# Attention units worked off in two halves, with value products between the turns, in a two-layer diffusion backbone kernel

## The reference, cut to what matters

```
o_b = softmax(q_b k_b^T) v_b            6 query heads on 2 key/value heads, 64 wide
o_c = rmsnorm((softmax(q_0 k_0^T) - lam * softmax(q_1 k_1^T)) v_c)    4 heads, 2 maps of 32
```

## Time and profile before

| What | us |
|---|---|
| median of 3 runs | 2925.51 (2918.04 to 2929.34) |
| the profiled execution, its own time | 2917.24 |
| its span, first to last instruction | 2915.6 |
| mean granted clock of TensorE in it | 0.903 of full speed |
| unit loop, layer 0 | 444.8 to 704.5 |
| unit loop, layer 1 | 1666.5 to 1929.9 |

### The profile page before, as it was taken

One profiled execution on the slowest core, in us unless ns is written; L12 is line 12 of the kernel. 1 busy time (PEld: TensorE's weight loads), 2 busy tenths in 40 slices (PEclk: granted clock), 3 DMA queues, 4 the chain that ended last, 5 costly groups with the idle time before them and its releaser, 6 DMA issues. The chain is left out here.

```text
span 2915.6 us, 46493 instructions
## 1 busy us (share of the span) xinstructions
PE 2488.3 (85%) x18972; PEld 2217.9 (76%) x18972; DVE 1454.1 (50%) x2077; ACT 1072.0 (37%) x1752; POOL 312.4 (11%) x334
## 2 busy tenths in 40 slices
PE   6995878776899999989949697777599999999993
PEld 4983655555899999989836565567499999999993
DVE  5675654555432223246656645543345555555556
ACT  4332244443322122143313535532235444444443
POOL 0064322000000000000643220000100000000002
PEclk8997986888999999999979868887699999999997
DMA  5324739101232222213146000010666765676664
GB/s 202 94 66 111 213 119 300 61 1 37 66 84 62 79 73 68 69 52 87 39 111 199 19 0 1 1 47 12 217 187 202 224 207 174 205 233 203 184 190 173
DMA packets 453114, 340.46 MB, mean 117 GB/s; under 512 B 90961, under 2 KB 421151, under 8 KB 451935
## 3 DMA queue, kind: packets, MB, share of 16 engines
q1 hardware_dynamic: 436383, 277.43, 32.9%
q10 hardware_dynamic: 11520, 41.95, 4.4%
q0 software_dynamic: 5056, 18.88, 1.7%
HBM read 287.68 MB, written 50.53 MB: 116 GB/s over the span
## 5 line engine op out<-in xcount | busy, mean ns | idle before, releaser
L2321 PE MATMUL ps<-h_hi,w_hi 128*128 128x256 f32 x1408 | 399.9, 284 | 5.6 <-DVE w_lo L2404 5.6
L2321 PE MATMUL ps<-h_lo,w_hi 128*128 128x256 f32 x1408 | 399.5, 284 | 0.0
L2321 PE MATMUL ps<-h_hi,w_lo 128*128 128x256 f32 x1408 | 399.4, 284 | 0.0
L2404 DVE TENSOR_TENSOR w_lo<-w_raw,w_hi 128x2048 fp32r<-128x2048 f32 (+1 forms) x180 | 309.2, 1756 | 120.6 <-ACT w_hi L2354 120.6
L2321 PEld LDWEIGHTS ps<-h_hi,w_hi 128*128 128x128 f32 x1408 | 271.0, 192 | 8.7 <-issue 6.0
L2321 PEld LDWEIGHTS ps<-h_lo,w_hi 128*128 128x128 f32 x1408 | 271.0, 192 | 2.8
L2321 PEld LDWEIGHTS ps<-h_hi,w_lo 128*128 128x128 f32 x1408 | 271.0, 192 | 0.0
L2354 ACT CAST w_hi<-w_raw 128x2048 fp32r<-128x2048 f32 (+1 forms) x180 | 256.6, 1474 | 2.6 <-DMA w_raw<-in_moe_w_down 2.6
L1829 DVE TENSOR_TENSOR p_lo<-ps,p_hi 128x512 fp32r<-128x512 f32 (+1 forms) x196 | 121.7, 632 | 136.5 <-ACT p_hi L1896 136.2
L1886 ACT ACTIVATE tm<-ps,tm 128x768 f32<-128x768 f32 (+1 forms) x140 | 111.3, 795 | 203.2 <-DVE tm L1824 203.1
L1824 DVE TENSOR_REDUCE tm<-ps 128x1 f32<-128x768 f32 (+1 forms) x140 | 113.1, 819 | 118.6 <-PE ps L1728 66.2
(11 more groups left out here) (427 smaller groups left out, 5624.6 us busy)
## 6 DMA issues: line engine op xcount, KB each, us to landing
w_raw<-in_moe_w_gu SPq DMA_DIRECT2D x182, 512.0 KB, 5.1
w_raw<-in_moe_w_down SPq DMA_DIRECT2D x91, 512.0 KB, 5.9
G_decay<-in_ada_w ACTq DMA_DIRECT2D x54, 512.0 KB, 4.7
w_ahead<-in_ffn_w_gu SPq DMA_DIRECT2D x44, 512.0 KB, 5.2
slots_h<-tm SPq DMA_DIRECT2D x13, 1024.0 KB, 11.1
slots_y<-tm SPq DMA_DIRECT2D x12, 1024.0 KB, 11.2
w_ahead<-in_ffn_w_down SPq DMA_DIRECT2D x16, 704.0 KB, 4.7
oA<-in_ada_w ACTq DMA_DIRECT2D x20, 512.0 KB, 5.0
```

Source lines behind the costliest of these rows:

```text
L2321: mm = pe.matmul(ps[:, j % 2, half * BLK:(half + 1) * BLK], gu(wt, j, half, k), x[:, k, :], start=(k == 0 and n == 0), stop=(k == KC - 1 a ...
L2404: dve.tensor_tensor(wlo[:, q, part], raw[:, q, part], whi[:, q, part].bitcast(F32), ALU.subtract).then_inc(s["lo_d" if down else "lo_u"], 1)
```

## The change

The unit's tiles get the order 1, 2, 3, 4, 0 (`order`). Tiles 1 and 2 are the first half, tiles 3 and 4 the second, each with its own half of `p_hi` and `p_lo` and its own half of the sums' bank; the context block has a place of its own behind both. The 12 products of 512 columns become 24 of 256 columns. In turn v, PE does the second half's products of unit v-1 and the first half's of unit v, two key blocks at a time, between turns and scores. `bring_out` waits for two halves. DVE and ACT orders follow; `probabilities` of a tile stands one tile later behind its scores. Beside that, `gdn` and `gdiff` are loaded in the preparing stage of attention into free columns of `mixed`, where `nlam` and `ro` now lie too, and `out_proj` copies `gdiff` into a buffer first.

```diff
-                    sp.dma_start(self.gdn[:], i["dn_norm"][l].partition_broadcast(P)).then_inc(s["par_in"], 16)
-                    sp.dma_start(self.gdiff[:], i["diff_norm"][l].partition_broadcast(P)).then_inc(s["par_in"], 16)
...
+                        sp.dma_start(gdn, i["dn_norm"][l].partition_broadcast(P)).then_inc(s["gain_in"], 16)
+                        sp.dma_start(gdiff, i["diff_norm"][l].partition_broadcast(P)).then_inc(s["gain_in"], 16)
...
-                        chain(dve.tensor_tensor(nlam[:], ls[:, 1:2], ls[:, 0:1], ALU.subtract))
-                        chain(dve.tensor_scalar(nlam[:], nlam[:], -lam_init, None, ALU.add))
-                        chain(dve.tensor_scalar(gdiff[:], gdiff[:], 1.0 - lam_init, None, ALU.mult))
+                        chain(dve.tensor_tensor(nlam, ls[:, 1:2], ls[:, 0:1], ALU.subtract))
+                        chain(dve.tensor_scalar(nlam, nlam, -lam_init, None, ALU.add))
+                        dve.wait_ge(s["gain_in"], 32)
+                        chain(dve.tensor_scalar(gdiff, gdiff, 1.0 - lam_init, None, ALU.mult))
...
-            p_hi, p_lo = sb("p_hi", [P, PL], F32R), sb("p_lo", [P, PL], F32R)
+            p_hi, p_lo = sb("p_hi", [P, PL + P], F32R), sb("p_lo", [P, PL + P], F32R)
...
-            STEPS = ((-1, ()), (0, ((0, 0), (0, 1), (0, 2), (0, 3))), (1, ((1, 0), (1, 1), (1, 2), (1, 3))),
-                     (1, ((0, 4), (1, 4), (0, 5), (1, 5))),
-                     (2, ((2, 0), (2, 1), (2, 2), (2, 3))), (3, ((3, 0), (3, 1), (3, 2), (3, 3))),
-                     (3, ((2, 4), (3, 4), (2, 5), (3, 5))))
-            NS = len(STEPS)
+            TILES = (1, 2, 3, 4, 0)
+            ITEMS = (((1, 0), (1, 1), (1, 2), (1, 3)), ((2, 0), (2, 1), (2, 2), (2, 3)), ((1, 4), (2, 4), (1, 5), (2, 5)), ((0, 0),),
+                     ((3, 0), (3, 1), (3, 2), (3, 3)), ((4, 0), (4, 1), (4, 2), (4, 3)), ((3, 4), (4, 4), (3, 5), (4, 5)))
+            NS = len(ITEMS)
+
+            def order(u, t):
+                return NT * u + TILES.index(t)
...
                     def turn(u, j):
                         n = NS * u + j
-                        pe.wait_ge(s["p_in"], NT * u + STEPS[j][0] + 2)
+                        pe.wait_ge(s["p_in"], max(order(u, t) for t, k in ITEMS[j]) + 1)
                         if n >= 2:
                             pe.wait_ge(s["lo"], n - 1)
...
-                    def weigh(u, k):
+                    def weigh(u, half, k):
 
                         if k == 0:
-                            pe.wait_ge(s["lo"], NS * (u + 1))
-                            if u == 0:
+                            pe.wait_ge(s["lo"], NS * u + (7 if half else 3))
+                            if half == 0 and u:
+                                pe.wait_ge(s["o_sb"], u)
+                            if half == 0 and u == 0:
                                 pe.wait_ge(s["v_lo"], NV)
-                            if u:
-                                pe.wait_ge(s["o_sb"], u)
+                        p0 = half * PL // 2 + k * 2 * P
                         for n, part in enumerate((p_hi, p_lo)):
-                            mm = pe.matmul(ps[:, OB, :], values(u, k + 1), part[:, k * 4 * P:(k + 1) * 4 * P],
+                            mm = pe.matmul(ps[:, OB, half * 2 * P:(half + 1) * 2 * P], values(u, k + 1), part[:, p0:p0 + 2 * P],
                                            start=(k == 0 and n == 0), stop=(k == NKL - 1 and n == 1))
                         if k == NKL - 1:
                             mm.then_inc(s["pv"], 1)
...
                     def weigh_context(u):
 
-                        pe.wait_ge(s["lo"], NS * u + 1)
+                        pe.wait_ge(s["lo"], NS * u + 4)
                         if u:
                             pe.wait_ge(s["o_out"], u)
-                            pe.wait_ge(s["o_ctx"], u)
-                        else:
-                            pe.wait_ge(s["v_lo"], NV)
                         for n, part in enumerate((p_hi, p_lo)):
-                            mm = pe.matmul(ps[:, XB, 0:P], values(u, 0), part[:, PL - P:PL], start=(n == 0), stop=(n == 1))
+                            mm = pe.matmul(ps[:, XB, 0:P], values(u, 0), part[:, PL:PL + P], start=(n == 0), stop=(n == 1))
                         mm.then_inc(s["pvc"], 1)
 
...
                     for v in range(-1, NU + 1):
                         ahead, now, done = v + 1 < NU, 0 <= v < NU, v >= 1
                         if ahead:
-                            scores(v + 1, 0)
                             scores(v + 1, 1)
+                        if now:
+                            turn(v, 0)
                         if done:
-                            for k in range(4):
-                                weigh(v - 1, k)
+                            weigh(v - 1, 1, 0)
+                            weigh(v - 1, 1, 1)
+                        if now:
+                            turn(v, 1)
                         if ahead:
                             scores(v + 1, 2)
                         if done:
-                            for k in range(4, NKL):
-                                weigh(v - 1, k)
+                            weigh(v - 1, 1, 2)
+                            weigh(v - 1, 1, 3)
                         if now:
-                            for j in range(3):
-                                turn(v, j)
+                            turn(v, 2)
+                        if done:
+                            weigh(v - 1, 1, 4)
+                            weigh(v - 1, 1, 5)
+                            weigh_context(v - 1)
+                        if now:
+                            turn(v, 3)
                         if ahead:
                             scores(v + 1, 3)
                         if now:
-                            turn(v, 3)
+                            turn(v, 4)
+                            weigh(v, 0, 0)
+                            weigh(v, 0, 1)
+                            turn(v, 5)
+                        if ahead:
+                            scores(v + 1, 4)
+                        if now:
+                            weigh(v, 0, 2)
+                            weigh(v, 0, 3)
                         if done:
                             turn_out(v - 1)
                         if now:
-                            turn(v, 4)
+                            turn(v, 6)
+                            weigh(v, 0, 4)
+                            weigh(v, 0, 5)
                         if ahead:
-                            scores(v + 1, 4)
-                        if now:
-                            weigh_context(v)
-                            turn(v, 5)
-                            turn(v, 6)
+                            scores(v + 1, 0)
...
                     for v in range(-1, NU + 1):
                         ahead, now, done = v + 1 < NU, 0 <= v < NU, v >= 1
+                        if now:
+                            split_lo(v, 0)
                         if ahead:
-                            for t in range(3):
-                                least(v + 1, t)
+                            least(v + 1, 1)
                         if now:
-                            for j in range(3):
-                                split_lo(v, j)
+                            split_lo(v, 1)
+                        if ahead:
+                            least(v + 1, 2)
+                        if now:
+                            split_lo(v, 2)
+                            split_lo(v, 3)
+                            split_lo(v, 4)
                         if ahead:
                             least(v + 1, 3)
                         if now:
-                            split_lo(v, 3)
+                            split_lo(v, 5)
+                        if ahead:
+                            least(v + 1, 4)
                         if done:
                             if v - 1 == HB:
                                 dve.wait_ge(s["gated"], 3 * NT)
                             out(v - 1)
                         if now:
-                            split_lo(v, 4)
+                            split_lo(v, 6)
                         if ahead:
-                            least(v + 1, 4)
-                        if now:
-                            split_lo(v, 5)
-                            split_lo(v, 6)
+                            least(v + 1, 0)
...
-                            act.wait_ge(s["turned"], NS * (u - 2) + 1)
+                            act.wait_ge(s["turned"], NS * (u - 2) + 4)
                         if t and n >= PR:
                             u0, t0 = divmod(n - PR, 4)
-                            act.wait_ge(s["turned"], NS * u0 + (4, 4, 7, 7)[t0])
+                            act.wait_ge(s["turned"], NS * u0 + (3, 3, 7, 7)[t0])
                         if t and n == PR - 1:
...
                     def split_hi(u, j):
                         n = NS * u + j
                         act.wait_ge(s["turned"], n + 1)
```

(55 more changed lines are left out.)

32 lines of the change are left out of this document (14 added, 18 removed).

## The result

The changed kernel takes 2810.72 us (median of 4 runs, 2805.11 to 2817.73) against 2926.93 for the kernel before (median of 4, one more than above): a ratio of 0.961 (95% interval 0.9575 to 0.9644), 116 us faster. The forecast was 2858, 67 us faster, with a range down to 2828. The direction and the place were right, the size was not.

The account below looks back on a forecast made before the run. Hand-overs between PE, DVE and ACT were taken to bound attention's loops, no engine being full. Layer 0 -31.9, layer 1 -35.4 and +0.4 for small edits made -67 us, from 2925.5 to 2858; range 2828 to 2896.

Parts of the forecast that it names:

- C turns: Attention's unit loops, eight turns a layer: a chain of 12.54 us each, 100.3 instead of 131.6; less 29.3 with slow entry.
- B turns: Attention's unit loops, four turns a layer: 18.3 us each, 73.2 for four; less 0.6 in layer 0, 4.1 in layer 1.
- I take 55%: B turns: assumed share of time at 2.4 GHz, mixing 15.4 and 23.9 us a turn into 18.3.
- rival 4: B units stay at 2.4 GHz too: 61.6 us, 12 and 15 us less in the layers, 2834 us; chance 12%.
- The ends: Each attention loop's last units less 4 us (0 to less 6), its start plus 2 (0 to plus 4).
- Small edits: Moved loads and waits: nothing, at most 1 us a layer; `gdiff` copy in the output projection plus 0.4 us in all.
- columns: Unit's products: 12 of 512 columns become 24 of 256, 0.12 us apart at 2.4 GHz, 2.88 us a unit.
- Rule against row: PE clock: profile rows show transposes lifting it; the Trainium skill says the full clock does not engage for transposes.
- 1: PE's queue in every unit: the clock never rises, C turns 18.0 us, +36 and +33 us, 2994 us; chance 8%.
- 5: Nothing moves, because one exponential per tile still gates two score slots: same time; chance 2%.
- 2: The clock keeps falling once a unit: C turns 14.1 us, less 19 instead of 29.3 a layer, 2879 us; chance 20%.
- 3: In-order queues block, S2 waiting for the context exponential: C turns 14.2 us, plus 13 a layer, 2885 us; chance 13%.

Follow-up runs that it names:

- filled kernel: The kernel before with six extra products of 512 columns per unit in the places where PE waited; 2917.0 us, ratio 0.999.
- runs kernel: The changed kernel with its halves kept, but each half's 12 products of 256 columns in one run; 2848.3 us, ratio 0.974.

## Why the prediction was wrong in size

**What bounds the kernel: right.** Nobody was full; the three engines handed on in a chain, and the wait for the last low part ahead of the products was its worst link.

**C turns: mechanism right, term mis-sized.** 12.54 us forecast, 12.00 measured. I let every copy, low part and high part hold its engine for its whole length, though the next instruction starts sooner; the four sections between the matmul groups above are each 0.06 to 0.22 shorter than priced. The entry at 1.2 GHz (plus 2) didn't happen, and the last of the eight intervals, already without scores, is 10.1. Together 8.1 us a layer, 16 of the missing 49. That the clock would stay up was forecast, but the figure for it was not like with like: the 63% set against the new order's 72% is PE's share of the ten us behind the products alone. Over the whole C stretch it was 70% before (92.1 of 131.6) and is 79% now (74.6 of 94.1).

**B turns: the step that failed.** "I take 55%" of the time at 2.4 GHz came from the clock of the kernel before and was carried over to an order that changes the clock. Measured are 100% in layer 1 (window 1.00) and all but one stretch of some 10 us (490.4 to 500.7) in layer 0 (0.92). The price at 2.4 GHz was good: 15.4 (its own sum, 12.54 + 3 x 0.98, is 15.48), measured 15.33 for two units in a row in layer 0 and three in layer 1. The 23.9 for 1.2 GHz is not shown: no B unit of the changed kernel ran at that clock throughout. The filled kernel's B units took as much, but with the old order, six products more and part of the time at 2.4 GHz, so that is a coincidence. Had I given B the argument that I gave C, the four turns would have been 61.6, which stood in the text as a bound and in rival 4 at 12%; they were 63.0 and 59.7. This is 24 us of the 49. So the share of 2.4 GHz is an outcome of the new order. The runs kernel shows that the place of the products decides it in C units; for B units no run shows what does. With the products in runs the four B turns took 63.3 us in layer 0, as in the changed kernel, and 67.7 in layer 1, and the kernel with one exponential moved lost the clock in three B units of layer 1. That the changed kernel kept it there is measured, not explained.

**The ends.** Less 3.4 for less 4, right. The start gave 3.3 us instead of costing 2: I saw the longer first exponential, and not that unit 0's twelve wide products no longer stand together in front of its copy (477.9 to 484 before, with one score tile between, eight of them at 1.2 GHz). The clock also rose sooner: it came up some 10 us ahead of the first copy-out in either layer, against under 4 before, and the start's mean clock is 0.64 instead of 0.54. This is read off the traces; no run tests it apart. Ten us over both layers.

The four parts make up the 49 us by which the medians miss. The spans miss by 45: the 5 us outside the loops went the other way.

**Small edits and columns: right**, each run alone, to within what a median can tell.

**Rule against row: the row held.** The clock rose behind transposes alone, and the rival that rested on the rule (2994 us) is out. The changed kernel is no test of transposes by themselves, since products stand between them. In the section of transposes and scores of the runs kernel the clock did fall, but PE was idle half of it.

**Rivals.** 1 and 5 are out. 2 did not come true for the change, but the runs kernel is it: C units of 12.0 and 14.5 to 14.8 us in turn. 3 is out: S2 did wait for the context exponential, 0.36 us in the unit shown (580.43). 4 was right about B; its 2834 us is still 23 too slow, by the C turns and the start.

Open: what lets the clock fall in B units, the place of the products or the load of PE; why some C units of the runs kernel lose it and others don't; how much of the shorter chain is the halves and how much the new orders of DVE and ACT.

## What to carry to other kernels

When a change alters how evenly PE is fed, its clock share is an outcome, not an input: don't take it from the old trace; work the time out for both levels and argue from the new gaps which one holds, for every stretch alike, and let the range take in the other. Walk the new order of all engines with start-to-start distances from rows; that walk gave each unit's length at 2.4 GHz to about half a us, and it names the next link to move (here one turn ahead of turn_out, another 20 us). An experiment whose time says "no change" may hold two effects that cancel; its units in the trace say more than its median.

## What was not expected of the hardware

The clock fell behind a stretch in which PE was still busy 1.76 of 3.40 us (runs kernel, 565.4 to 568.8), with no wait of PE longer than 1.13 us there, and it stayed up over the same stretch of other units. One kernel in one execution can hold 2.4 GHz over B units in one layer and lose it in the other (the exponential moved: 1.00 and 0.80). And work that is there only to keep it up is unreliable: it held over three B units in layer 0 and over none in layer 1 of the same execution, and 4.0 us of dense products at a loop's start (nine in a row from 451.06) bought less than 7 us of 2.4 GHz.
